# Last work item of the expert layer: its rows put in their places by a 0/1 matrix on TensorE and stored plainly, not scattered by GpSimd

## What is computed

```python
def moe_swiglu(u, w_router, b_router, w_gate, w_up, w_down):
    ...
    def expert_block(args):
        tok, e = args
        xb = xt[tok]
        hb = jax.nn.silu(xb @ w_gate[e]) * (xb @ w_up[e])
        return hb @ w_down[e]
    ...
    y_slots = y_slots.reshape(P, D) * slot_w[:, None].astype(u.dtype)
    return jnp.zeros((T, D), u.dtype).at[slot_tok].add(y_slots).reshape(B, L, D)

# in reference():
            h = h + moe_swiglu(u, w_router[i], b_router[i], w_exp_gate[i], w_exp_up[i], w_exp_down[i])
    return h[:, N_META:]
```

## Time and profile before

| what | us |
|---|---|
| median of 3 runs | 1798.14 (1797.11 to 1798.52) |
| the profiled execution | 1786.34 |
| its span (first to last instruction) | 1784.5 |
| TensorE busy in the span | 1722.4 (97%) |
| mean granted TensorE clock | 0.986 of full speed |
| last matmul ends, on the span's clock | 1773.02 |

### The profile page before, as it was taken

How to read it: one execution, slowest core, us unless ns; L and a number is a source line. 1 busy time by engine, 2 the same in 40 slices (tenths; PEclk the granted TensorE clock), 3 DMA queues, 4 the chain that set the end, 5 groups by cost and what they waited for, 6 DMA issues and landing times.

```text
span 1784.5 us, 50784 instructions
## 1 busy us (share of the span) xinstructions
PE 1722.4 (97%) x22518; PEld 1402.3 (79%) x22518; DVE 675.5 (38%) x1307; ACT 580.3 (33%) x1190; POOL 123.8 (7%) x126
## 2 busy tenths in 40 slices
PE   8999999999998999999999999999999999999997
PEld 7989889999997988889876665666767756555797
DVE  7758677777546768777200010010100101001010
ACT  6768776543345786874200000000000000000000
POOL 0000001100020000002110102002010020110200
PEclk9999999999999999999899999999999999999998
DMA  6323334555554433336999999999999999999992
GB/s 222 130 95 133 116 106 143 165 171 173 167 176 154 132 120 130 130 121 239 416 411 419 381 413 381 410 405 368 407 382 409 409 375 414 391 403 412 362 418 87
DMA packets 89910, 486.09 MB, mean 272 GB/s; under 512 B 12684, under 2 KB 15660, under 8 KB 46416
## 3 DMA queue, kind: packets, MB, share of 16 engines
q1 hardware_dynamic: 83936, 476.12, 69.3%
q0 software_dynamic: 5616, 6.57, 1.7%
q10 hardware_dynamic: 144, 0.13, 0.0%
HBM read 476.65 MB, written 7.40 MB: 271 GB/s over the span
## 4 chain that ended last, share of the span: by engine, by line
PE 87%; ACT 5%; DVE 4%; issue 3%; DMA 0%; SPq 0%; POOLq 0%; POOL 0%; ACTq 0%; DVEq 0%
PE bank L1903 33%; PE bank L1920 16%; PE bank L1590 10%; PE bank L1592 10%; PE bank L1591 10%; ACT hi L727 1%; PE bank L1666 1%; PE bank L1781 1%; PE bank L1784 1%; PE bank L1706 1%; PE bank L1759 1%; DVE lo L1038 1%; PE bank L1770 1%; ACT ez L764 0%; PE bank L1878 0%
## 5 line engine op out<-in xcount | busy, mean ns | idle before, releaser
L1903 PE MATMUL bank<-chunk,xt 128*32 128x256 f32 x10752 | 592.0, 383 | 23.3 <-issue 22.5
L1903 PEld LDWEIGHTS bank<-chunk,xt 128*32 128x32 f32 x10752 | 412.5, 111 | 202.4 <-issue 34.7
L1590 PE MATMUL bank<-UH,hi 128*128 128x272 f32 (+1 forms) x1024 | 308.6, 301 | 9.4 <-DVE UL L1051 5.7
L1592 PE MATMUL bank<-UH,lo 128*128 128x272 f32 (+1 forms) x1024 | 294.4, 287 | 0.0
L1591 PE MATMUL bank<-UL,hi 128*128 128x272 f32 (+1 forms) x1024 | 293.6, 287 | 0.0
L1920 PE MATMUL bank<-chunk,turned_hs 128*32 128x256 f32 x5376 | 292.3, 379 | 0.0
L1539 DVE TENSOR_TENSOR hs<-sg,bank 128x512 f32<-128x512 f32 x24 | 16.5, 688 | 726.1 <-PE bank L1903 726.1
L1038 DVE TENSOR_TENSOR lo<-raw,hi 128x1024 fp32r<-128x1024 f32 (+1 forms) x220 | 265.6, 1212 | 42.8 <-ACT hi L727 42.4
L1920 PEld LDWEIGHTS bank<-chunk,turned_hs 128*32 128x32 f32 x5376 | 205.0, 110 | 85.6
L727 ACT ACTIVATE hi<-raw 128x1024 fp32r<-128x1024 f32 (+1 forms) x220 | 229.3, 1043 | 107.7 <-PE bank L1592 106.6
L1590 PEld LDWEIGHTS bank<-UH,hi 128*128 128x128 f32 x1024 | 193.7, 189 | 20.8 <-issue 16.2
(11 more groups left out here) (334 smaller groups left out, 1781.3 us busy)
## 6 DMA issues: line engine op xcount, KB each, us to landing
chunk<-in_w_exp SPq DMA_DIRECT2D x336, 1024.0 KB, 8.3
raw<-in_w_dense SPq DMA_DIRECT2D x212, 512.0 KB, 3.3
raw<-in_w_dense SPq DMA_DIRECT2D x8, 384.0 KB, 3.1
wuq<-in_w_uq SPq DMA_DIRECT2D x2, 1024.0 KB, 8.7
hT<-in_tokens SPq DMA_DIRECT2D x4, 272.0 KB, 3.7
wukv<-in_w_ukv SPq DMA_DIRECT2D x2, 512.0 KB, 9.2
y_rows<-acc SPq DMA_DIRECT2D x1, 1024.0 KB, 18.2
u_rows<-u_strips SPq DMA_DIRECT2D x1, 1024.0 KB, 18.7
```

The source lines that it names most:

```text
L1590: MM(ps, h, xh_, start=first, stop=False)
L1592: return MM(ps, l, xh_, start=False, stop=last)
L1903: ins = MM(bank[b_ + t // 2][q * ROWS:(q + 1) * ROWS, t % 2 * DQ:(t % 2 + 1) * DQ], xt[:, t, kt0 + r, :], w_[:, (r * NQ + q) * DQ:(r * NQ ...
```

## The change

GpSimd does nothing for the last item after `next_rows`. SyncE loads the 256 token rows of `y_rows` into `acc` (L626 of the changed kernel), as two blocks `b` of 128 tokens, one a partition. VectorE makes from the item's row numbers a 0/1 matrix `home`: for each group t and block b, partition (q, slot) has a 1 in the column of its token. The token is the row number divided by 4 less `strip_no`, a constant column of (p // 32) / 4. TensorE then multiplies `home` (32 partitions of quarter q, 128 columns) by `ysb` of quarter q (32 partitions, 256 columns), summed over the three groups, into `bank[4b + q]`: 24 matmuls after the loop. VectorE adds each result to `acc` and SyncE stores `acc` to `out` in four pieces of 256 KB. `y_last`, the indirect gathers, the indirect scatters and the DRAM copy are gone.

```diff
@@ -623,10 +623,13 @@
             sp.wait_ge(rows_added, n_before + 1)
-            sp.dma_start(out[0].rearrange("(p r) d -> p (r d)", p=P),
-                         y_whole[0:SEQ, :].rearrange("(p r) d -> p (r d)", p=P)).then_inc(out_stored, 16)
-            sp.wait_ge(out_stored, 16)
-            sp.wait_ge(rows_stored, 16 * N_T)
+            sp.dma_start(acc[:], y_whole[0:SEQ, :].rearrange("(b p) d -> p b d", p=P)).then_inc(y_loaded, 16)
+            for b in range(2):
+                for half in range(2):
+                    sp.wait_ge(last_made, 4 * b + 2 * half + 2)
+                    sp.dma_start(out[0, b * P:(b + 1) * P, half * 512:(half + 1) * 512],
+                                 acc[:, b, half * 512:(half + 1) * 512]).then_inc(out_stored, 16)
+            sp.wait_ge(out_stored, 64)
@@ -700,15 +703,6 @@
             next_rows(n_before)
-            for t in range(N_T):
-                pool.indirect_dma_start(y_last[:, t, :], None, y_rows[:],
-                                        bass.IndirectOffsetOnAxis(rows[:, t, 0:1], 0)).then_inc(y_gathered, 16)
-            pool.wait_ge(out_stored, 16)
-            for t in range(N_T):
-                pool.wait_ge(last_made, t + 1)
-                pool.indirect_dma_start(out[0].rearrange("r (q c) -> (r q) c", q=NQ),
-                                        bass.IndirectOffsetOnAxis(rows[:, t, 0:1], 0), ysum[:, t, :], None,
-                                        bounds_check=SEQ * NQ - 1, oob_is_err=False).then_inc(rows_stored, 16)
@@ -1557,11 +1551,25 @@
             dve.wait_ge(this_made, n_items)
-            dve.wait_ge(y_gathered, 16 * N_T)
-            dve.wait_ge(h_stored, 32)
-            for t in range(N_T):
-                dve.wait_ge(y_made, n_items * N_T + (t + 1))
-                TT(ysum[:, t, :], ysb[:, t, :], y_last[:, t, :], ALU.add).then_inc(last_made, 1)
+            st(CP(tok_f[:, 0, :], rows[:, 0:N_T, 0]))
+            st.wait()
+            st(TS(tok_f[:, 0, :], tok_f[:, 0, :], 1.0 / NQ, strip_no, ALU.mult, ALU.subtract))
+            st.wait()
+            st(TS(tok_f[:, 1, :], tok_f[:, 0, :], float(P), None, ALU.subtract))
+            st.wait()
+            for b in range(2):
+                for t in range(N_T):
+                    ins = TS(home[:, t, b * P:(b + 1) * P], iota, tok_f[:, b, t:t + 1], None, ALU.is_equal)
+                    if (b, t) == (1, N_T - 1):
+                        ins.then_inc(home_made, 1)
+                    else:
+                        st(ins)
+            dve.wait_ge(y_loaded, 16)
+            for b in range(2):
+                dve.wait_ge(y_home, b + 1)
+                for q in range(NQ):
+                    c = slice(q * DQ, (q + 1) * DQ)
+                    TT(acc[:, b, c], acc[:, b, c], bank[4 * b + q][:, 0:DQ], ALU.add).then_inc(last_made, 1)
@@ -1924,6 +1932,15 @@
+            pe.wait_ge(home_made, 1)
+            for b in range(2):
+                for t in range(N_T):
+                    pe.wait_ge(y_made, n_items * N_T + (t + 1))
+                    for q in range(NQ):
+                        ins = MM(bank[4 * b + q][:, 0:DQ], home[q * ROWS:(q + 1) * ROWS, t, b * P:(b + 1) * P],
+                                 ysb[q * ROWS:(q + 1) * ROWS, t, :], start=t == 0, stop=t == N_T - 1)
+                ins.then_inc(y_home, 1)
```

More of the change, by code:

```diff
@@ L439, in bass_hybrid_trunk @@
         ysb = sb("ysb", [P, N_T, DQ])
-        y_last = sb("y_last", [P, N_T, DQ])
+        home = sb("home", [P, N_T, SEQ])
         xtok = sb("xtok", [P, D])
@@ L450, in bass_hybrid_trunk @@
         nit_i = sb("nit_i", [1, 2], I32)
-        pairs = sb("pairs", [P, 2 * N_T, 2])
+        pairs, tok_f = sb("pairs", [P, 2 * N_T, 2]), sb("tok_f", [P, 2, N_T])
         u_strips = sb("u_strips", [P, 2, NQ, KD, ROWS])
-        late = sb("late", [P, 2924])
+        late = sb("late", [P, 2918])
         chunk = [sb(f"chunk{i}", [P, 2048]) for i in range(MRAW)]
@@ L457, in bass_hybrid_trunk @@
         pair = sb("pair", [P, 2, 2, PAIR_W])
+        strip_no = MC[:, 2 * P + NE:2 * P + NE + 1]
         iota, tri, least = MC[:, 0:P], MC[:, P:2 * P], MC[:, 2 * P:2 * P + NE]
@@ L463, in bass_hybrid_trunk @@
         u_whole_rows = u_rows.rearrange("(r q) c -> r (q c)", q=NQ)
-        ysum = acc[:].rearrange("p b d -> p (b d)")[:, 0:N_T * DQ].rearrange("p (t c) -> p t c", t=N_T)
         y_rows = nc.dram_tensor("y_rows", (3 * P * NQ, DQ), F32, kind="Internal").ap()
@@ L505, in bass_hybrid_trunk @@
         y_made = sem("y_made")
-        y_gathered = sem("y_gathered")
-        out_stored, rows_stored, last_made = sem("out_stored"), sem("rows_stored"), sem("last_made")
+        y_loaded, home_made, y_home = sem("y_loaded"), sem("home_made"), sem("y_home")
+        out_stored, last_made = sem("out_stored"), sem("last_made")
         class Steps:
@@ L1954, in constants @@
     moe[:, 2 * P] = -1
+    moe[:, 2 * P + NE] = p // ROWS / NQ
     return out, moe
```

## The result

The changed kernel took 1790.19 us (median of 5 runs, 1786.08 to 1791.61), the kernel before 1798.52 us (5 runs, 1797.11 to 1800.64): ratio 0.9943, 95% interval 0.9929 to 0.9957. It is faster by 8 to 10 us, not by 2.9 us.

What follows compares the result with a forecast made beforehand. TensorE, busy 97% of the span, bounds the kernel, with GpSimd's drain setting the end. The new tail sums to 1781.63 against 1784.5, 2.9 us less: median 1795.2 us, 0.16% faster, range 1793.8 to 1800.2.

Steps and rivals of the forecast that it cites:

- The drain: Program's end: GpSimd's DRAIN behind the scatters sets the end, 3.5 us after their landing; those 3.5 us go.
- the drain does not go: Program's end: the 3.5 us belong to the handshake, not the scatters; end 0.5 us later, 1798.6 us; chance 6%.
- leaving the loop costs: TensorE's loop exit costs as much as going round; matmuls start at 1775.87, half clock, 2.0 us more; chance 6%.
- TensorE side by side: After the loop: four 32-row matmuls run at once, 48 records at 53.5 ns each, block 1 ready at 1776.59.
- my forecast's own range: Whole kernel: 1794.4 us (landing 2.1 us, additions 0.34 us apart) to 1796.2 us (landing 3.3 us, slower matmuls).
- Weight loads bind: New matmuls: 128-column loads share one path, 0.11 us a record; only 0.5 us less, 1797.6 us; chance 14%.
- No side by side: New matmuls: 32-row ones run one after another, 0.216 us a record; 4.6 us more, 1802.7 us; chance 13%.
- The rest of the tail: After the loop: matmuls, eight additions to 1778.33, last store landing at 1781.13, then 0.25 and 0.25 us to 1781.63.
- The landing of the last store: SyncE's last store at the end: 2.7 us, from a 512 KB load's 3.3 us less 0.6 us for half the bytes.
- The gathers lay beside 80 us of matmuls: 0: Last item: removing GpSimd's three gathers of 0.95 us each gains 0, as they lie beside matmuls.
- I expect nothing from the stretch before 1773 us: Before the loop's end: TensorE waits for neither the removed gathers nor the DRAM copy, so no gain there.
- the 11.8 us: Whole kernel: the median of the runs shown lies 11.8 us over the profiled execution; 2.9 us was subtracted from that median.

Runs made afterwards that it cites:

- the run that forced it: Changed kernel with all 24 matmuls of the 0/1 matrix reading partitions 0 to 31: 1802.89 us, ratio 1.0032 to the kernel before.

## Why the prediction was right or wrong

- **The drain** was read rightly. It was what ended last in the tail, the change took it away, and one late scatter brings back 3.3 us of tail. The rivals "the drain does not go" and "leaving the loop costs" fell: the new matmuls start 0.70 us after the loop's last.
- **TensorE side by side**: right, 2.87 us for 48 records against my 23 x 0.0535 + 0.38 + 1.28 = 2.89. The ratio of 3.07 that the Trainium skill gives in "TensorE: Matmul & The Clock Gate", section "Packing small matmuls — row/col tiling", stood for an estimated 3.3 us in place of 2.6; it was on the upper end of my forecast's own range. The trace has 2.5 us from the first record's start to the last one's (2.87 less the 0.38 of the last record), and the measurement decides. "Weight loads bind" (0.107 us a record) fell as well, since 2.5 us for 47 steps are 0.053. "No side by side" did not come true, but the run that forced it shows that four quarters are needed and that my price was some 6 us too low (13.9 us over the changed kernel, not 7.5), since the clock falls.
- **The rest of the tail** was sized too long: I had 8.6 us, it is 7.7. The landing of the last store is 2.1 us, not 2.7: the row of a 512 KB load was the wrong neighbour, and the 2.4 us of the small scatters the nearer one. The additions come at 0.33 us, not 0.365: (2.73 - 0.41) / 7. This moved 2.9 to 3.75 us.
- **"The gathers lay beside 80 us of matmuls: 0"**, and with it "I expect nothing from the stretch before 1773 us", is the step that failed. Three more indirect gathers behind the item's own three cost 3.6 us (kept in the changed kernel) or 4.3 us (spread in the kernel before). The weights were not late: in the run with the gathers kept, the chunk that TensorE was in when it slowed had landed at 1657.4 and was begun at 1687.5. It is TensorE's issue that slows. Tail 3.75 us and burst 3.6 to 4.3 us make 7.4 to 8.0 us, against 8.5 and 10.2 us measured by the two ratios (0.9953 and 0.9943); the intervals of these two ratios are 2.5 to 3.4 us to either side, so nothing more is shown to be missing. The price of the burst is no sharper than that either.
- **Why I did not see it**: the execution that I read was one in which the burst did no harm. The last item took 109.3 us there; it took 114.3 us in the second profile of the same kernel. The sign that I had was the 11.8 us between that execution and the median. I subtracted from it instead of asking which stretch differs from run to run. With the second profile beside it the answer is plain: there every item has a dip at its own three gathers, and the last item has the longest.

What stays open is how a burst of indirect gathers reaches TensorE. Shown: LDWEIGHTS and MATMUL come late together; a matmul record is 0.38 to 0.40 us long at full clock, as ever; the wait view names no semaphore ("issue"); in the runs with six more gathers it holds whether rows are 1 KB or 256 B. In the slowed stretch TensorE's records come in bunches, in the second profile of before at 1693.32, 1694.74 and 1696.18. The 16 KB packets of the instruction queue (q8), 6.2 to 7.5 us apart from 1684 to 1746 us in the first profile, where TensorE runs freely, are 11.2 us apart there (1689.95 and 1701.18) and 14.0 us apart in the run with six more gathers (1684.90 and 1698.93). That can be the cause of the slow issue or follow from it. That TensorE's instructions themselves arrive late would fit all of this, and so would another path shared with GpSimd's indirect DMAs. No run here separates them.

## What to carry to other kernels

Work of GpSimd at the very end is dearer than its landing: look at the DRAIN rows of the program's end, and have SyncE issue the last stores. That TensorE does not wait for indirect gathers does not make them free. In a kernel with TensorE always busy, spread them: here that gave 7 to 9 us on top of the change, about as much as the change itself. On the kernel before only the three gathers of the last item were spread. And if the one execution you read is 0.7% from the median, find out which stretch varies before you price anything against it.

## What the hardware showed that I had not expected

- Six indirect gathers back to back cut TensorE's issue rate to about a third for 6 us (36 records in 6 us, against 112), nine for 9 us and longer; one alone does nothing, and three plain GpSimd loads behind the item's own gathers do nothing beyond what those do (0.8 to 0.9 us). One execution of 14 showed none of this, for a reason that stays open.
- The granted clock fell from 2.4 to 1.2 GHz while TensorE was 100% busy, when all its matmuls used 32 of the 128 rows, one at a time. With four side by side, in the changed kernel, it stayed at full, but that is no comparison: those matmuls took 2.87 us in all, and in the run in one quarter the clock was still full over the first 3.3 us (1777.68 to 1781.0).
- GpSimd's DRAIN behind late scatters lasts 7.4 to 7.9 us whether there are three or one. Where the DMA queues are still full of weights it lasts longer (11.75 us in the changed kernel, from 1686.0 on), but there nothing waits for it.
